# Weighted value sums of three of eight decode samples computed by VectorE, and the value ring cut from three slots to two

## The chip, the cores and the metric

The kernel runs on one core of one Trainium2 chip. The metric is the device time of one launch in microseconds (us); lower is better. Three runs of the kernel before gave 2659.47, 2661.23 and 2663.26 us, so the median is 2661.23 us.

## The reference, cut to what matters

One decoder layer is applied to a prompt of 512 tokens and to eight samples of one new token each. The change touches only the samples' attention over their cached pages:

```python
# D_MODEL 2048, SEQ 512, DEC_BATCH 8, PAST_LEN 1024, PAGE_SIZE 128, SB_HEADS 8, HEAD_DIM 128
k_past = cache_k[i][page_table].reshape(dec_b, past_len, SB_HEADS, HEAD_DIM)
v_past = cache_v[i][page_table].reshape(dec_b, past_len, SB_HEADS, HEAD_DIM)
...
def stick_breaking(q, k, v, sb_bias, q_pos, k_pos):
    z = einsum('bqhd,bkhd->bhqk', q, k) * SB_SCALE + sb_bias
    log_keep = where(causal, log_sigmoid(-z), 0.0)
    after = cumsum(log_keep, axis=3, reverse=True) - log_keep
    a = where(causal, exp(log_sigmoid(z) + after), 0.0)
    return einsum('bhqk,bkhd->bqhd', a, v)
```

For one sample and one head the last line is a sum over 1024 cached positions: weight `a` times the 128 numbers of that position's value row. A page holds 128 positions (one per partition) and eight heads of 128 numbers, so a page in SBUF is 128 x 1024 fp32, 512 KB, and a sample has eight pages. Around it stand the combined input projection, the prompt's attention, a gated position-mixing MLP, the output projection, a SwiGLU feed-forward layer of width 5632 and an embedding gate.

## The kernel before, in words

**Units.** The dense layers are cut into units of 16 weight blocks of 128 x 128. Every block is multiplied in three passes (`x_hi`·`w_hi`, `x_lo`·`w_hi`, `x_hi`·`w_lo`, two halves of 260 tokens each, line 1214). TensorE walks through the units in order. Units 0 to 7 make the queries, 8 to 23 the MLP channels, 24 to 39 keys and values (`U_KV` is 24), from 40 on the output projection follows (`U_OUT` is 40). The feed-forward layer starts at unit 56.

**Turns.** Every other engine has one block of code per unit, in a program order that was written by hand. Below, "turn u" is what an engine does in its loop's round u. VectorE's turn u begins with reading the result tile of unit u-1 (`take`, line 892), for which it waits until TensorE has ended that unit. Then come `low_w` (line 868: the low halves of the weights of unit u+1, without which TensorE can't begin unit u+1), the MLP's or the attention's element-wise steps, and the scoring of cached keys. So TensorE can be ahead of VectorE by at most about one unit. In the even turns of the key and value units VectorE waits for ScalarE's softplus (`soft`, line 958), in the odd ones for TensorE's sums over later positions (line 971).

**Cached keys.** VectorE scores each key page with a product and a reduction (lines 899, 900): three pages per turn in turns 10 to 23, two per turn in turns 24 to 34. The query rows of the next sample arrive by a DMA (`q_rows`) that may be issued only when the last page of the sample before has been scored.

**Cached values.** `V_FIRST = [16, 19, 22, 25, 28, 31, 34, 38]` gives the unit in which the pages of each sample begin: three pages in that unit, three in the next and two in the third. In a unit with three pages `weigh_values` puts them ahead of blocks 7, 11 and 14. It takes each head's 128 x 128 values as the weights of a matmul with one column, eight heads per page, in fp32, which the trace shows as 16 weight loads and 16 matmuls (line 1336). VectorE then reads eight columns of sums out of PSUM at the start of its next turn (`take_values`, lines 937, 940).

**The value ring and GpSimd's queue.** GpSimd issues the loads of value pages. There are three slots: two in `v_ring` and the tile `acc`, which in turn 9 carries the query rows to DRAM. The load of page j waits until page j-3 has been used. GpSimd also squares and adds up finished outputs for the norms (lines 553, 554). Its program is one list, sorted by these keys, and it is worked off strictly in that order:

```python
jobs = [(v_unit(j - V_SLOTS) + 0.8, "load", j) for j in range(V_SLOTS, N_PAGES)]
jobs += [(U_MLP + 3.5 + 2 * i, "mlp", i) for i in range(HEADS)]
jobs += [(U_KV + 3.7 + 2 * i, "attention", i) for i in range(HEADS)]
```

An "attention" job i waits for the head's output. TensorE computes that output in unit 27 + 2i ahead of block 12 (`attend`, lines 1317 and 1321), and ScalarE copies it to `q` (line 660).

Of the kernel before, what the change touches and what calls it, by code (L numbers as in the profile page):

```python
# [26 lines left out]
P = 128  # L27
# [94 lines left out]
V_SLOTS = 3  # L122
# [13 lines left out]
V_UNITS = [u for u in range(V_FIRST[0], V_FIRST[-1] + 3) if v_pages(u)]  # L136
# [27 lines left out]
def build(nc, w_units, x_t, p_t, cache_k, cache_v, page_table, g_mix, g_out, g_ffn, g_ple, g_q, g_k,  # L164
# [3 lines left out]
    with ExitStack() as ctx:  # L168
# [101 lines left out]
        def v_slot(j):  # L270

            return acc[:, :] if j % V_SLOTS == RING else v_ring[:, j % V_SLOTS, :]

        def o_s_ps(u):

            return out_ps[:, 2 * ((tiles_before(u + 1) - 1) % 2) + 1, HALF:HALF + HEADS]
# [68 lines left out]
        v_used = sem("v_used")  # L345
        v_read = sem("v_read")
# [14 lines left out]
        av_ready = sem("av_ready")  # L361

# [19 lines left out]
        def _(sp):  # L382
# [51 lines left out]
            for u in range(U_FFN):  # L434
# [25 lines left out]
                if u == V_UNITS[-1] + 2:  # L460

                    sp.wait_ge(v_used, N_PAGES)
                    sp.dma_start(h[:, H_KEYS:H_PAGES, :], x_t[:, H_KEYS:H_PAGES, :]).then_inc(h_in[1], 16)
# [22 lines left out]
        def _(pool):  # L486
# [112 lines left out]
        def _(act):  # L599
# [71 lines left out]
            def weights_of_sample(u):  # L671

                if u - 1 in SUM_END:
                    b = SUM_END.index(u - 1)
                    act.wait_ge(arg_s_done, b + 1)
                    if b >= 3:
                        act.wait_ge(v_used, PAGES * (b - 2))
# [177 lines left out]
        def _(dve):  # L855
# [73 lines left out]
            def take_values(u):  # L929

                if u not in V_UNITS:
                    return
                b = v_pages(u)[0] // PAGES
                dve.wait_ge(out_done, tiles_before(u + 1))
                sums = q[:, :, PROMPT + b]
                if u == V_FIRST[b]:
                    dve.tensor_copy(sums, o_s_ps(u)).then_inc(v_read, 1)
# [72 lines left out]
            for u in range(1, U_FFN):  # L1010
# [104 lines left out]
                while pages:  # L1115
                    score_next()
                if u > U_OUT_SB:
# [89 lines left out]
        def _(pe):  # L1207
# [117 lines left out]
            def weigh_values(j, u):  # L1325
# [6 lines left out]
                if j == pages[0] and V_UNITS.index(u) > 1:  # L1332
                    pe.wait_ge(v_read, V_UNITS.index(u) - 1)
                for hd in range(HEADS):
                    at = pg * HEADS + hd
                    mm = pe.matmul(o_s_ps(u)[:, hd:hd + 1], v_slot(j)[:, hd * P:(hd + 1) * P],  # L1336
                                   a_s[:, b % 3, at:at + 1], start=False, stop=j == pages[-1],
                                   skip_group_check=True)
                mm.then_inc(v_used, 1)

# [15 lines left out]
            for u in range(1, U_FFN):  # L1356
# [31 lines left out]
                for at, j in zip((14, 11, 7), reversed(v_pages(u))):  # L1388
                    between[at] = lambda j=j, u=u: weigh_values(j, u)
# [148 lines left out]
```

## Time and profile before

| | |
|---|---|
| median of three runs | 2661.23 us |
| the profiled execution's own time | 2663.89 us |
| its span | 2662.3 us |
| TensorE busy | 2623.2 us, 99% |
| VectorE busy | 1218.7 us, 46% |
| ScalarE busy | 781.3 us, 29% |
| GpSimd busy | 158.2 us, 6% |
| chain that ended last | TensorE 95%, VectorE 3%; line 1214 87%, line 1336 4% |

The span is the profiled time from the first to the last instruction of the core, 1.6 us under that execution's own time. Busy shares are means over the whole launch. The change acts only between about 240 and 740 us, so the views that matter are those of this stretch: VectorE's instructions in order of time with the idle time before each, and the same of GpSimd and TensorE. In a row of such a view the first number is the start, the second the duration of the row (several instructions of one kind are merged, with their count at the end), and the bracket says how long the engine sat idle before it and for whom.

### The profile page before, as it was taken

The page shows a single profiled execution, that of the slowest core. Times are in us where ns is not written, and L with a number is a line of the kernel's source. Part 1 is how long each engine was busy: PE and PEld are TensorE (multiplying, and loading weights), DVE is VectorE, ACT ScalarE, POOL GpSimd, SP SyncE. Part 2 cuts the span into 40 slices and gives each one's busy share as a digit, 9 for nine tenths or more (in the row PEclk, how much of TensorE's full clock was granted, in tenths as well). Part 3 has the DMA queues.
Part 4 walks back from the last instruction along what each step waited for, and adds up shares of the span by engine and source line. Part 5 has one row for each costly group of instructions (what it writes and reads, how often), then busy time and mean ns, then how long its engine had stood idle before and what let it go on. Part 6 is the DMA issues. An engine that isn't in the chain of part 4 may idle for free.

```text
span 2662.3 us, 49219 instructions
## 1 busy us (share of the span) xinstructions
PE 2623.2 (99%) x21484; PEld 2600.7 (98%) x21484; DVE 1218.7 (46%) x1400; ACT 781.3 (29%) x912; POOL 158.2 (6%) x170
## 2 busy tenths in 40 slices
PE   7999999999999999999999999999999999999999
PEld 6998999999999999999999999999999999999999
DVE  6368776554456533333333333334343424346443
ACT  5544434444523322222122212121212121224221
POOL 4001111110111200000000000000000000003000
PEclk9998999999999999999999999999999999999999
DMA  4255565554332222222222222222222222222223
GB/s 177 95 190 190 215 237 207 175 186 160 108 128 100 84 96 95 85 91 96 96 82 93 96 80 96 96 96 81 95 96 92 93 86 96 94 83 94 96 86 106
DMA packets 57389, 309.18 MB, mean 116 GB/s; under 512 B 7770, under 2 KB 7770, under 8 KB 30178
## 3 DMA queue, kind: packets, MB, share of 16 engines
q1 hardware_dynamic: 47826, 272.50, 29.0%
q0 software_dynamic: 9216, 33.56, 3.6%
q8 instruction: 177, 2.90, 0.4%
q14 instruction: 26, 0.21, 0.0%
q10 hardware_dynamic: 144, 0.01, 0.0%
HBM read 297.46 MB, written 8.59 MB: 115 GB/s over the span
## 4 chain that ended last, share of the span: by engine, by line
PE 95%; DVE 3%; DMA 1%; ACT 1%; issue 1%; SPq 0%; DVEq 0%; ACTq 0%
PE out_ps L1214 87%; PE out_ps L1336 4%; PE pair_ps L1253 1%; DVE w_lo L868 1%; DVE k_ring L899 0%; PE tok_ps L1321 0%; DVE dot_s L900 0%; DMA q_rows<-q_rows_dram 0%; DMA h<-x_t 0%; ACT x_hi L622 0%; PE pair_ps L1284 0%; PE pair_ps L1303 0%; PE tok_ps L1317 0%; PE pair_ps L1290 0%; PE pair_ps L1299 0%
## 5 line engine op out<-in xcount | busy, mean ns | idle before, releaser
L1214 PE MATMUL out_ps<-x_hi,w_hi 128*128 128x260 f32 x5184 | 1066.9, 287 | 25.8 <-DVE w_lo L868 10.0
L1214 PE MATMUL out_ps<-x_hi,w_lo 128*128 128x260 f32 x5184 | 1048.6, 284 | 0.0
L1214 PE MATMUL out_ps<-x_lo,w_hi 128*128 128x260 f32 x5184 | 1046.8, 284 | 0.0
L1214 PEld LDWEIGHTS out_ps<-x_hi,w_hi 128*128 128x128 f32 x5184 | 805.8, 190 | 31.8 <-DVE w_lo L868 8.9
L1214 PEld LDWEIGHTS out_ps<-x_hi,w_lo 128*128 128x128 f32 x5184 | 803.6, 189 | 0.0
L1214 PEld LDWEIGHTS out_ps<-x_lo,w_hi 128*128 128x128 f32 x5184 | 801.4, 189 | 0.0
L611 ACT ACTIVATE w_hi<-w_raw 128x1024 fp32r<-128x1024 f32 x412 | 411.7, 1047 | 590.2 <-PE out_ps L1214 590.2
L868 DVE TENSOR_TENSOR w_lo<-w_raw,w_hi 128x1024 fp32r<-128x1024 f32 x410 | 501.4, 1255 | 125.1 <-ACT w_hi L611 123.7
L1214 PE MATMUL out_ps<-act_hi,w_lo 128*128 128x260 f32 x1408 | 283.9, 283 | 0.0
L1214 PE MATMUL out_ps<-act_lo,w_hi 128*128 128x260 f32 x1408 | 283.3, 283 | 0.0
L1214 PE MATMUL out_ps<-act_hi,w_hi 128*128 128x260 f32 x1408 | 283.2, 282 | 0.0
L1156 DVE TENSOR_TENSOR h<-h,out_ps 128x520 f32<-128x520 f32 x176 | 122.3, 695 | 228.2 <-PE out_ps L1214 228.1
L1214 PEld LDWEIGHTS out_ps<-act_hi,w_lo 128*128 128x128 f32 x1408 | 217.1, 188 | 0.0
L1214 PEld LDWEIGHTS out_ps<-act_hi,w_hi 128*128 128x128 f32 x1408 | 217.1, 188 | 0.0
L1214 PEld LDWEIGHTS out_ps<-act_lo,w_hi 128*128 128x128 f32 x1408 | 216.6, 188 | 0.0
L1131 DVE TENSOR_TENSOR y_up<-out_ps,h_r 128x520 f32<-128x520 f32 x44 | 30.8, 700 | 295.6 <-PE out_ps L1214 295.6
L1131 DVE TENSOR_TENSOR y_gate<-out_ps,h_r 128x520 f32<-128x520 f32 x44 | 30.8, 700 | 285.0 <-PE out_ps L1214 285.0
L818 ACT ACTIVATE act_hi<-y_up 128x520 fp32r<-128x520 f32 x44 | 28.1, 639 | 428.2 <-DVE y_up L1148 428.2
L815 ACT ACTIVATE y_gate<-y_gate 128x520 f32<-128x520 f32 x44 | 28.1, 640 | 381.5 <-DVE y_gate L1131 381.5
L593 POOL COPY h_sum<-h_sq 128x520 f32<-128x520 f32 x2 | 1.8, 902 | 1543.8 <-ACT h_sq L691 1543.8
L1336 PEld LDWEIGHTS out_ps<-a_s,v_ring 128*128 128x128 f32 x688 | 82.1, 195 | 0.0
L1336 PE MATMUL out_ps<-a_s,v_ring 128*128 128x1 f32 x688 | 80.7, 247 | 0.0
(175 smaller groups left out, 1366.0 us busy)
## 6 DMA issues: line engine op xcount, KB each, us to landing
w_raw<-w_units SPq DMA_DIRECT2D x205, 1024.0 KB, 4.8
k_ring<-cache_k SPq DMA_DIRECT2D x50, 512.0 KB, 5.2
v_ring<-cache_v POOLq DMA_DIRECT2D x43, 512.0 KB, 4.5
acc<-cache_v POOLq DMA_DIRECT2D x21, 512.0 KB, 4.8
k_third<-cache_k SPq DMA_DIRECT2D x14, 512.0 KB, 4.5
h<-x_t SPq DMA_DIRECT2D x4, 1040.0 KB, 9.5
y_t<-h SPq DMA_DIRECT2D x16, 260.0 KB, 6.5
q_rows<-q_rows_dram SPq DMA_DIRECT2D x8, 512.0 KB, 5.4
```

The source lines that it names most:

```text
L593: ins = pool.tensor_copy(h_sum[:, :], h_sq[:, 0, :])
L611: act.activation(w_hi[:, u % 2, cols], w_raw[:, u % 2, cols], ACT.Copy).then_inc(hi_done, 1)
L815: act.activation(y_gate[:, :], y_gate[:, :], ACT.Silu).then_inc(silu_done, 1)
L818: act.activation(act_hi[:, par, g, :], y_up[:, :], ACT.Copy).then_inc(act_hi_done, 1)
L868: dve.tensor_tensor(w_lo[:, u % 2, cols], w_raw[:, u % 2, cols], w_hi[:, u % 2, cols], ALU.subtract).then_inc(lo_done, 1)
L1131: dve.tensor_tensor(halves(dst), tile_ps(t), halves(h_r[:, :]), ALU.mult).then_inc(out_read, 1)
L1156: dve.tensor_tensor(halves(h[:, m, :]), halves(h[:, m, :]), tile_ps(t), ALU.add)\
L1214: mm = pe.matmul(out_ps[:, 2 * (t % 2) + a, 0:HALF], w[:, u % 2, cols], x[:, a * HALF:(a + 1) * HALF], start=first and n == 0, stop=last a ...
L1253: mm = pe.matmul(pair_ps[:, a, 0:HALF], ones[:, :], x[:, a * HALF:(a + 1) * HALF], start=True, stop=True)
L1336: mm = pe.matmul(o_s_ps(u)[:, hd:hd + 1], v_slot(j)[:, hd * P:(hd + 1) * P], a_s[:, b % 3, at:at + 1], start=False, stop=j == pages[-1], s ...
```

## The change

`BY_VECTOR = (1, 3, 5)` names the samples whose value pages VectorE takes. For each of their pages `add_page` multiplies the whole page in place by the weights, which are broadcast over the 128 numbers of a head, and adds it to `acc` (copies it for the first page). It stands at the end of VectorE's turn, behind the last scoring of keys. One unit after the last page, `reduce_values` lets TensorE sum `acc` over the partitions: eight matmuls of one column with `ones`, of the same form as those of a page. `acc` is no longer a slot of the ring, and `V_SLOTS` goes from 3 to 2. The other five samples keep their blocks and units. ScalarE's wait for a free weight tile goes to `v_weighed` where VectorE was the reader.

```diff
-V_SLOTS = 3
+V_SLOTS = 2
...
+BY_VECTOR = (1, 3, 5)
+BY_TENSOR = [b for b in range(SAMPLES) if b not in BY_VECTOR]
+V_UNITS = sorted([(V_FIRST[b] + i, b) for b in BY_TENSOR for i in range(3)] + [(V_FIRST[b] + 3, b) for b in BY_VECTOR])
...
         def v_slot(j):
 
-            return acc[:, :] if j % V_SLOTS == RING else v_ring[:, j % V_SLOTS, :]
+            return v_ring[:, j % V_SLOTS, :]
...
                 if j >= V_SLOTS:
-                    pool.wait_ge(v_used, j - V_SLOTS + 1)
-                elif j % V_SLOTS == RING:
-                    pool.wait_ge(q_rows_out, 16)
+                    before = j - V_SLOTS
+                    if before // PAGES in BY_VECTOR:
+                        pool.wait_ge(v_added, used_by_vector(before))
+                    else:
+                        pool.wait_ge(v_used, used_by_tensor(before))
...
+            def add_page(j):
+
+                b, pg = divmod(j, PAGES)
+                dve.wait_ge(v_in[j % V_SLOTS], 16 * (j // V_SLOTS + 1))
+                values = v_slot(j).rearrange("p (h d) -> p h d", h=HEADS)
+                weights = a_s[:, b % 3, pg * HEADS:(pg + 1) * HEADS].unsqueeze(2).to_broadcast([P, HEADS, P])
+                if pg == 0:
+                    dve.wait_ge(a_s_done, b + 1)
+                    if b == BY_VECTOR[0]:
+                        dve.wait_ge(q_rows_out, 16)
+                    else:
+                        dve.wait_ge(acc_used, BY_VECTOR.index(b))
+                chained(dve.tensor_tensor(values, values, weights, ALU.mult), v_weighed)
+                if pg == 0:
+                    dve.tensor_copy(acc[:, :], v_slot(j)).then_inc(v_added, 1)
                 else:
-                    dve.wait_ge(v_read, V_UNITS.index(u))
-                    dve.tensor_tensor(sums, sums, o_s_ps(u), ALU.add).then_inc(v_read, 1)
+                    dve.wait_ge(v_added, used_by_vector(j) - 1)
+                    dve.tensor_tensor(acc[:, :], acc[:, :], v_slot(j), ALU.add).then_inc(v_added, 1)
...
                 while pages:
                     score_next()
+                for j in v_pages(u):
+                    if j // PAGES in BY_VECTOR:
+                        add_page(j)
...
+            def reduce_values(b, u):
+
+                pe.wait_ge(v_added, used_by_vector(PAGES * b + PAGES - 1))
+                pe.wait_ge(v_read, V_UNITS.index((u, b)) - 2)
+                for hd in range(HEADS):
+                    mm = pe.matmul(o_s_ps(u, b)[:, hd:hd + 1], acc[:, hd * P:(hd + 1) * P], ones[:, 0:1],
+                                   start=False, stop=True, skip_group_check=True)
+                mm.then_inc(acc_used, 1)
...
                 for at, j in zip((14, 11, 7), reversed(v_pages(u))):
-                    between[at] = lambda j=j, u=u: weigh_values(j, u)
+                    if j // PAGES in BY_TENSOR:
+                        between[at] = lambda j=j, u=u: weigh_values(j, u)
+                for b in BY_VECTOR:
+                    if u == V_FIRST[b] + 3:
+                        between[13] = lambda b=b, u=u: reduce_values(b, u)
```

The order of the instructions moves at two places that matter below. VectorE, end of turn 19 and start of turn 20, before (the names: `k_third` is a slot of the key ring, `y` the tile that `take` fills):

```order
L899 TENSOR_TENSOR k_ring<-k_ring,q_rows 128x1024 [waits k_in1,centred]
L900 TENSOR_REDUCE dot_s<-k_ring 128x8 [waits vec_step]
L899 TENSOR_TENSOR k_third<-k_third,q_rows 128x1024 [waits k_in2]
L900 TENSOR_REDUCE dot_s<-k_third 128x8 [waits vec_step]
L937 COPY q<-out_ps 128x8 [waits out_done]
L892 TENSOR_TENSOR y<-out_ps,x_r 128x520 [waits out_done]
```

and of the change at the same place:

```order
L921 TENSOR_TENSOR k_third<-k_third,q_rows 128x1024 [waits k_in2]
L922 TENSOR_REDUCE dot_s<-k_third 128x8 [waits vec_step]
L975 TENSOR_TENSOR v_ring<-v_ring,a_s 128x1024 [waits q_rows_out,a_s_done,v_in0]
L977 COPY acc<-v_ring 128x1024 [waits v_weighed]
L975 TENSOR_TENSOR v_ring<-v_ring,a_s 128x1024 [waits v_in1]
L980 TENSOR_TENSOR acc<-acc,v_ring 128x1024 [waits v_added,v_weighed]
L975 TENSOR_TENSOR v_ring<-v_ring,a_s 128x1024 [waits v_in0]
L980 TENSOR_TENSOR acc<-acc,v_ring 128x1024 [waits v_added,v_weighed]
L914 TENSOR_TENSOR y<-out_ps,x_r 128x520 [waits out_done]
```

Six wide instructions now stand ahead of the next turn's reading of TensorE's tile. The third page uses slot 0 again, which the first page of the same turn has only just left.

GpSimd, around the "attention" job 1 (unit 29), before. The two loads ahead of the job are those of pages 36 and 37 (pages 4 and 5 of sample 4), the load behind it, which goes to the slot `acc`, is that of page 38:

```order
L548 DMA v_ring<-cache_v 128x1024
L543 TENSOR_LOAD table
L543 ISA x2
L548 ISA [waits v_used]
L548 DMA v_ring<-cache_v 128x1024
L553 TENSOR_TENSOR pool_sq<-q 128x512 [waits tok_read]
L554 TENSOR_TENSOR sb_r<-sb_r,pool_sq 128x512 [waits pool_step]
L543 TENSOR_LOAD table [waits pool_step]
...
L548 DMA acc<-cache_v 128x1024
```

and of the change, where the load behind the job is that of page 37:

```order
L567 DMA v_ring<-cache_v 128x1024
L572 TENSOR_TENSOR pool_sq<-q 128x512 [waits tok_read]
L573 TENSOR_TENSOR sb_r<-sb_r,pool_sq 128x512 [waits pool_step]
L560 TENSOR_LOAD table [waits pool_step]
L560 ISA x2
L567 ISA [waits v_used]
L567 DMA v_ring<-cache_v 128x1024
```

Page 37 is the third page of unit 29. Its load has gone from ahead of the job to behind it, since its key is now made from page 35, which belongs to unit 29 itself. The same happens to page 53 in unit 35 (job 4) and to page 61 in unit 39 (job 6).

## Rows read from the trace of the kernel before

**Rows 1.** The page: VectorE's busy tenths in 40 equal slices of the span.

```profile
DVE  6368776554456533333333333334343424346443
```

**Rows 2.** The chain of waits in order of time: start, us, what; one page.

```profile
313.49 1.68 PE out_ps L1336 x16
```

**Rows 3.** VectorE's groups by line and shape, 0 to 760 us: busy, mean ns.

```profile
L899 DVE TENSOR_TENSOR k_ring<-k_ring,q_rows 128x1024 f32<-128x1024 f32 x50 | 61.2, 1224 | 13.3 <-DMA q_rows<-q_rows_dram 9.0 <-DMA k_ring<-cache_k 3.0
...
L977 DVE TENSOR_TENSOR z<-z,causal 128x512 f32<-128x512 f32 x8 | 5.5, 687 | 5.0 <-ACT z L755 3.6 <-ACT z L781 1.4
```

**Rows 4.** VectorE in order of time: first instructions of turns 20 to 22.

```profile
320.69 0.17 DVE L937 COPY q<-out_ps 128x8 f32<-128x8 f32 x1 [3.45 <-PE out_ps L1214]
...
338.68 1.22 DVE L899 TENSOR_TENSOR k_third<-k_third,q_rows 128x1024 f32<-128x1024 f32 x1 [7.57 <-DMA q_rows<-q_rows_dram]
...
341.08 0.16 DVE L940 TENSOR_TENSOR q<-q,out_ps 128x8 f32<-128x8 f32 x1
...
355.69 0.17 DVE L940 TENSOR_TENSOR q<-q,out_ps 128x8 f32<-128x8 f32 x1 [1.10 <-PE out_ps L1214]
```

**Rows 5.** The same view: first instructions of turns 26 to 28.

```profile
428.36 0.17 DVE L937 COPY q<-out_ps 128x8 f32<-128x8 f32 x1 [7.23 <-PE out_ps L1214]
...
447.90 0.17 DVE L940 TENSOR_TENSOR q<-q,out_ps 128x8 f32<-128x8 f32 x1 [2.80 <-PE out_ps L1214]
...
469.49 0.17 DVE L940 TENSOR_TENSOR q<-q,out_ps 128x8 f32<-128x8 f32 x1 [6.36 <-PE out_ps L1214]
```

**Rows 6.** The same view: first instructions of turns 32 to 34.

```profile
553.91 0.17 DVE L937 COPY q<-out_ps 128x8 f32<-128x8 f32 x1 [8.13 <-PE out_ps L1214]
...
573.43 0.17 DVE L940 TENSOR_TENSOR q<-q,out_ps 128x8 f32<-128x8 f32 x1 [0.63 <-PE out_ps L1214]
...
595.52 0.17 DVE L940 TENSOR_TENSOR q<-q,out_ps 128x8 f32<-128x8 f32 x1 [6.66 <-PE out_ps L1214]
```

**Rows 7.** The same view: waits inside turns 26, 27 and 32.

```profile
437.50 1.49 DVE L958 SCALAR_TENSOR_TENSOR keep<-z,soft 128x1280 f32<-128x1280 f32 x1 [3.16 <-ACT soft L669]
...
452.77 1.22 DVE L971 TENSOR_TENSOR z<-z,pair_ps 128x1024 f32<-128x1024 f32 x1 [1.33 <-PE mix_ps L1309]
...
563.63 1.49 DVE L958 SCALAR_TENSOR_TENSOR keep<-z,soft 128x1280 f32<-128x1280 f32 x1 [3.75 <-ACT soft L669]
```

**Rows 8.** A page used by TensorE, GpSimd's next load, landing times of v_ring loads.

```profile
245.86 1.84 PE L1336 MATMUL out_ps<-a_s,v_ring 128*128 128x1 f32 x16
...
248.37 0.59 POOL L548 DMA_DIRECT2D v_ring<-cache_v  x1 [13.50 <-PE out_ps L1336]
...
DMA to landing us min/median/max: 3.4/4.5/8.2
```

**Rows 9.** Unit 29: GpSimd's attention job and next load; TensorE's third page.

```profile
508.85 1.04 POOL L553 TENSOR_TENSOR pool_sq<-q 128x512 f32<-128x512 f32 x1 [20.29 <-ACT q L660]
509.97 1.27 POOL L554 TENSOR_TENSOR sb_r<-sb_r,pool_sq 128x512 f32<-128x512 f32 x1
512.46 0.59 POOL L548 DMA_DIRECT2D acc<-cache_v  x1 [1.22 <-issue]
...
509.41 1.84 PE L1336 MATMUL out_ps<-a_s,v_ring 128*128 128x1 f32 x16
```

**Rows 10.** TensorE in order of time, unit 19: its first and its third page.

```profile
308.69 1.84 PE L1336 MATMUL out_ps<-a_s,acc 128*128 128x1 f32 x16
...
317.27 1.84 PE L1336 MATMUL out_ps<-a_s,v_ring 128*128 128x1 f32 x16
```

**Rows 11.** TensorE in order of time, behind a wait of 4.49 us.

```profile
202.41 2.10 PE L1253 MATMUL pair_ps<-vg,ones 128*128 128x260 f32 x4 [4.49 <-ACT vg L731]
...
208.63 0.42 PE L1214 MATMUL out_ps<-x_lo,w_hi 128*128 128x260 f32 x2
```

**Rows 12.** VectorE in order of time: `low_w` alone, and beside GpSimd's squares.

```profile
326.11 2.36 DVE L868 TENSOR_TENSOR w_lo<-w_raw,w_hi 128x1024 fp32r<-128x1024 f32 x2
...
376.36 4.35 DVE L868 TENSOR_TENSOR w_lo<-w_raw,w_hi 128x1024 fp32r<-128x1024 f32 x2
```

More of the change, by code:

```diff
@@ L133, in v_pages, with used_by_vector, used_by_tensor @@
     return [j for j in range(SAMPLES * PAGES) if v_unit(j) == u]
-V_UNITS = [u for u in range(V_FIRST[0], V_FIRST[-1] + 3) if v_pages(u)]
+BY_VECTOR = (1, 3, 5)
+BY_TENSOR = [b for b in range(SAMPLES) if b not in BY_VECTOR]
+V_UNITS = sorted([(V_FIRST[b] + i, b) for b in BY_TENSOR for i in range(3)] + [(V_FIRST[b] + 3, b) for b in BY_VECTOR])
+V_LAST = V_UNITS[-1][0]
+def used_by_vector(j):
+    return len([i for i in range(j + 1) if i // PAGES in BY_VECTOR])
+def used_by_tensor(j):
+    return j + 1 - used_by_vector(j)
 DIAG = lambda kb: slice(kb * P, (kb + 1) * P)
@@ L929, in take_values @@
             def take_values(u):
[L931 to L937, printed above, removed]
-                else:
-                    dve.wait_ge(v_read, V_UNITS.index(u))
-                    dve.tensor_tensor(sums, sums, o_s_ps(u), ALU.add).then_inc(v_read, 1)
+                for n, (v_u, b) in enumerate(V_UNITS):
+                    if v_u == u:
+                        dve.wait_ge(out_done, tiles_before(u + 1))
+                        sums = q[:, :, PROMPT + b]
+                        if b in BY_VECTOR or u == V_FIRST[b]:
+                            dve.tensor_copy(sums, o_s_ps(u, b)).then_inc(v_read, 1)
+                        else:
+                            dve.wait_ge(v_read, n)
+                            dve.tensor_tensor(sums, sums, o_s_ps(u, b), ALU.add).then_inc(v_read, 1)
+            def add_page(j):
[7 more added lines that the diff above has]
+                        dve.wait_ge(q_rows_out, 16)
+                    else:
+                        dve.wait_ge(acc_used, BY_VECTOR.index(b))
+                chained(dve.tensor_tensor(values, values, weights, ALU.mult), v_weighed)
+                if pg == 0:
+                    dve.tensor_copy(acc[:, :], v_slot(j)).then_inc(v_added, 1)
+                else:
+                    dve.wait_ge(v_added, used_by_vector(j) - 1)
+                    dve.tensor_tensor(acc[:, :], acc[:, :], v_slot(j), ALU.add).then_inc(v_added, 1)
             def weigh_sample(b):
@@ L1331, in weigh_values @@
                 pe.wait_ge(v_in[j % V_SLOTS], 16 * (j // V_SLOTS + 1))
[L1332 to L1333 removed]
+                n = V_UNITS.index((u, b))
+                if j == pages[0] and n > 2:
+                    pe.wait_ge(v_read, n - 2)
                 for hd in range(HEADS):
                     at = pg * HEADS + hd
[L1336 removed]
+                    mm = pe.matmul(o_s_ps(u, b)[:, hd:hd + 1], v_slot(j)[:, hd * P:(hd + 1) * P],
                                    a_s[:, b % 3, at:at + 1], start=False, stop=j == pages[-1],
```

16 lines of the change are left out of this document (11 added, 5 removed).

## The prediction

> **What bounds the kernel now.** I read the page first. TensorE is busy for 99% of the span, so in the mean only what leaves its queue counts. But the change acts between 240 and 740 us, and there VectorE is not idle: slices 4 to 7 of the page (each 66.6 us, so 200 to 466 us) show it six to eight tenths busy, against three or four in the feed-forward layer [rows 1]. That one number makes the page's mean of 46% useless for this question.
>
> So I went to VectorE's instructions in order of time and looked at the first one of each turn, because the bracket there says how long VectorE had nothing to do before TensorE ended the unit. That is the room the change has. In turns 19, 20 and 21, where sample 1's values are summed, the room is 3.45, nothing and 1.10 us [rows 4]. Turn 20 has none because VectorE waits 7.57 us inside it for the next sample's query rows, which come by DMA [rows 4]. In turns 25 to 27 (sample 3) the room is 7.23, 2.80 and 6.36 us [rows 5], in turns 31 to 33 (sample 5) 8.13, 0.63 and 6.66 us [rows 6].
>
> **What the change takes away.** The chain of waits gives 1.68 us of TensorE for a page [rows 2]. 24 of 64 pages leave it, 40.3 us, and three reductions of the same form come back, 5.0 us. If nothing else happened the gain would be 35.3 us. I do not add this number to the sum. It would be right only if TensorE set the pace of these nine units, and the next step shows that it does not.
>
> **What it adds to VectorE's turns.** A page is one multiply and one add of 128 x 1024 fp32 with both inputs in SBUF. The product in the scoring of keys is the same operation and takes 1.22 us [rows 3]. That one input is broadcast does not matter: the broadcast mask over 512 columns takes 0.69 us [rows 3], so 1024 columns would take no more than 1.4. I take 2.45 us for a page. The copy of a first page I leave at the add's price; at half of it a sample would be 0.6 us cheaper.
>
> In a turn with three pages the third one must wait. With two slots, its load can be issued only when the first page has been added. GpSimd starts a load 0.67 us after a page is released (TensorE ends at 247.70, the load starts at 248.37) and it lands 4.5 us later in the median, 3.4 to 8.2 at the ends [rows 8]. That is 5.2 us, and the second page covers 2.45 of it. VectorE idles 2.7 us (1.6 to 6.4 at the ends). A turn with three pages grows by 7.35 + 2.7 = 10.05 us, one with two pages by 4.9, a sample by 25.0.
>
> From then on VectorE sets the pace. `take` of the next turn stands behind the pages, and TensorE can only be one unit ahead: it needs the low weights made in that late turn. The turns add up end to end:
>
> - Sample 1: 25.0 - 3.45 - 0 - 1.10 = **+20.5 us**.
> - Sample 3: 25.0 - 7.23 - 2.80 - 6.36 = 8.6. With turns this late, TensorE's scores and ScalarE's softplus of turn 26, which don't need VectorE's `take`, are ready before VectorE asks. So the 3.16 us wait inside turn 26 goes, and the 1.33 us one in turn 27 too [rows 7]. **+4.1 us**.
> - Sample 5: 25.0 - 8.13 - 0.63 - 6.66 = 9.6, less 3.75 [rows 7] and 1.33 again, 4.5. In turn 31 the third page's load stands behind attention job 2, which waits for TensorE's head in the same unit. I put 2 us on that, between none and 4. **+6.5 us**.
>
> Together +31.1 us. The q_rows wait of 7.57 us stays in full, because `add_page` stands behind the key pages that wait for it and so fills none of it.
>
> **GpSimd beside it.** The squares of attention jobs 0, 2 and 3 (turns 27, 31, 33) now fall beside busy stretches of VectorE. They last 1.04 + 1.27 = 2.3 us [rows 9]. What such company costs is shown by a pair of `low_w`: 2.36 us alone, 4.35 beside GpSimd's squares of the MLP [rows 12]. I take 1 us for each job, **+3 us** (between 0 and 7). The Trainium skill (page "SBUF — State Buffer", section "SBUF: two separate sides") says that the port pair shared by the two engines is an exclusive lock, held for a whole instruction, when VectorE's op has two SBUF inputs and GpSimd's reads SBUF: the other one blocks fully. By that rule the three jobs would cost all of their 7 us if VectorE is always the one that waits, and the total would be 4 us higher. The doubled `low_w` pair agrees with the rule in direction. It also speaks against this change in general: two more two-input operations per page sit on that port.
>
> **The reductions.** Three times 1.68 us of TensorE in units 22, 28 and 34. TensorE has some lead when VectorE's late turns end, but the first page behind them must wait for a slot VectorE has just left (5.2 us after its release, as above). I call it even, **0 us** (between -4 and +5).
>
> **What two slots do to the samples that stay.** A third page's load now waits for the first page of the same unit. From the end of the first page to the start of the third are 317.27 - (308.69 + 1.84) = 6.7 us [rows 10], less 0.67 for GpSimd leaves 6.0 us for a landing of 4.5, at worst 8.2 [rows 8]. In units 16, 17, 22, 23, 28, 34 and 38 I take **+1 us** in all (0 to 6).
>
> Units 29, 35 and 39 are another matter. The load of their third page now has a key behind the attention job of the same unit, as the order in the section on the change shows. That job waits for the head that TensorE computes ahead of block 12, and the page is wanted ahead of block 14. The trace of before has all of it: the job is done at 511.24, the next load starts at 512.46, and TensorE's third page started at 509.41 [rows 9]. So the load starts 3.05 us after the page was wanted. I add a landing of 4.0 us, between 3.4 and the median, since little else is loaded then: 7.05 us of idle TensorE, in a stretch where TensorE is the bound. The other two units have the same spacing. **+21.2 us**.
>
> TensorE then comes back slower. After an idle 4.49 us it ran at half speed from 202.41 to about 208.63 [rows 11], 6.2 us that did 3.1 us of work. Three times 3.1 is **+9.3 us** (0 to 15). At VectorE's turns the same slowing has cover, since TensorE idles there anyway.
>
> **The sum.** 31.1 + 3 + 0 + 1 + 21.2 + 9.3 = 65.6 us on the profiled execution's 2663.9 us, 2729.5. That execution was 2.7 us above the median of its runs, so I forecast 2726.8, say **2727 us**. A measurement of this kernel can tell some 0.2%, 5.3 us, from no change.
>
> **The rivals.**
>
> 1. *VectorE's pages find cover (other side).* TensorE stays the bound of units 19 to 33, VectorE's idle time takes the pages, and 35.3 us go: 2626 us. It decides at the room per turn: 10 us are needed in six turns, 4.9 in three. For it speaks only the page's mean of 46%. Against it, no turn has 10 us of room and turn 20 has none [rows 4 to 6]. Chance 0.03.
> 2. *VectorE as forecast, but no stall in units 29, 35 and 39.* If something lets those loads through before block 14, 21.2 + 9.3 us drop out: 2696 us. Against it stands GpSimd's strict order. Chance 0.13.
> 3. *Loads land late.* Value, key and weight loads meet at the ends of VectorE's turns. If VectorE's six third pages land in 8.2 us and not in 4.5 [rows 8], 6 x 3.7 = 22 us come on top: 2749 us. Chance 0.12.
> 4. *Everything half-hidden, within 5.3 us of before.* It needs rival 2 and some 30 us less from VectorE's turns. Chance 0.02.
>
> My forecast has the remaining 0.70. Its own bounds (landings, port, clock) are about 2705 to 2750. The range that leaves out no more than 2 in 10 takes in rival 2 and most of rival 3: **2694 to 2752 us**. Faster by over 0.2% is rival 1, 0.03; within 0.2% is rival 4, 0.02; slower is the rest, 0.95.
>
> **What would show it.** Right, if in the profile after: no bracket stands before the first instruction of turns 20 to 22, 26 to 28 and 32 to 34; VectorE waits about 3 us for a load of `v_ring` in six places; the wait for `soft` is gone in turns 26 and 32; turns 20 and 21 together last some 50 us in place of the 35.0 between 320.69 and 355.69 [rows 4]; and TensorE shows three waits of about 7 us for a `v_ring` load, with a granted clock of one half behind each. Wrong, if TensorE's idle time stays near that of before, or if the three 7 us waits are missing (then rival 2, and my reading of GpSimd's order was mistaken), or if VectorE's turns do not add up end to end. I would also be wrong if the multiply by broadcast weights took much over 1.2 us: each 0.1 us of it is 2.4 us.

## The result and the profile after

The changed kernel took 2730.06 us (median of 4 runs, 2724.45 to 2731.66) against 2661.61 us of the kernel before (2659.47 to 2663.26). The ratio is 1.0251, with a 95% interval of 1.0238 to 1.0264: **slower by 68 us**, 3 us over the forecast of 2727. The profiled execution took 2729.34 us, its span is 2727.8 us, which is 65.5 us more than the span before. The sum in the prediction was 65.6.

The page after: the engines' totals, the slices and the chain.

```profile
PE 2620.9 (96%) x21148; PEld 2594.9 (95%) x21148; DVE 1278.2 (47%) x1442; ACT 781.3 (29%) x912; POOL 160.9 (6%) x170
...
PE   7999877988999999999999999999999999999999
...
DVE  6368778575445653343334343424243424336533
...
PEclk8998989898999999999999999999999999999999
...
PE 88%; DVE 7%; DMA 3%; issue 2%; POOL 0%; ACT 0%; SPq 0%; POOLq 0%; DVEq 0%; ACTq 0%
```

Some 35 us of TensorE's work left, yet it is busy for 2620.9 us against 2623.2: half clock filled in what the change took out. From 300 to 800 us TensorE worked at half clock for some 60 us, which is 30 us of work (read off windows of 0.5 us). VectorE's slices 7, 9 and 10 rose, from 6, 5 and 4 tenths to 8, 7 and 5 [rows 1], and 7% of the chain is VectorE now, 3% DMA, against 3% and 1%.

VectorE in order of time, from the first value page in turn 19 to the start of turn 22 (start, duration, and in the bracket the idle time ahead):

```profile
317.96 1.22 DVE L975 TENSOR_TENSOR v_ring<-v_ring,a_s 128x1024 f32<-128x1024 f32 x1
319.21 0.69 DVE L977 COPY acc<-v_ring 128x1024 f32<-128x1024 f32 x1
319.82 1.22 DVE L975 TENSOR_TENSOR v_ring<-v_ring,a_s 128x1024 f32<-128x1024 f32 x1
321.07 1.23 DVE L980 TENSOR_TENSOR acc<-acc,v_ring 128x1024 f32<-128x1024 f32 x1
324.07 1.22 DVE L975 TENSOR_TENSOR v_ring<-v_ring,a_s 128x1024 f32<-128x1024 f32 x1 [1.78 <-DMA v_ring<-cache_v]
...
326.48 0.69 DVE L914 TENSOR_TENSOR y<-out_ps,x_r 128x520 f32<-128x520 f32 x1
...
341.65 1.23 DVE L921 TENSOR_TENSOR k_third<-k_third,q_rows 128x1024 f32<-128x1024 f32 x1 [5.09 <-DMA q_rows<-q_rows_dram]
...
350.60 1.23 DVE L975 TENSOR_TENSOR v_ring<-v_ring,a_s 128x1024 f32<-128x1024 f32 x1 [1.68 <-DMA v_ring<-cache_v]
...
353.00 0.69 DVE L914 TENSOR_TENSOR y<-out_ps,x_r 128x520 f32<-128x520 f32 x1
...
371.13 0.69 DVE L914 TENSOR_TENSOR y<-out_ps,x_r 128x520 f32<-128x520 f32 x1
```

The turns begin with the `y<-out_ps` rows, and no bracket stands before them, where [rows 4] had 3.45, nothing and 1.10. A page costs 2.45 us, as forecast. The third page waits 1.78 and 1.68 us for its load.

TensorE in order of time, three of its long waits (units 21, 27 and 29):

```profile
354.42 2.10 PE L1296 MATMUL pair_ps<-vg,ones 128*128 128x260 f32 x4 [11.40 <-ACT vg L753]
...
475.55 2.07 PE L1296 MATMUL pair_ps<-sq,ones 128*128 128x260 f32 x4 [12.30 <-DVE z L1011]
...
538.94 3.57 PE L1380 MATMUL out_ps<-a_s,v_ring 128*128 128x1 f32 x16 [6.45 <-DMA v_ring<-cache_v]
```

And what released it: GpSimd in unit 29, the counterpart of [rows 9].

```profile
531.77 1.03 POOL L572 TENSOR_TENSOR pool_sq<-q 128x512 f32<-128x512 f32 x1 [22.34 <-ACT q L679]
532.88 1.26 POOL L573 TENSOR_TENSOR sb_r<-sb_r,pool_sq 128x512 f32<-128x512 f32 x1
535.36 0.59 POOL L567 DMA_DIRECT2D v_ring<-cache_v  x1 [1.22 <-issue]
```

The load of the third page starts at 535.36, behind the job, and lands 3.6 us later, when TensorE goes on at 538.94. The page then takes 3.57 us instead of the 1.84 of [rows 9]: TensorE is at half speed. Units 35 and 39 repeat it with 6.33 and 6.57 us.

Windows of the turns 19, 20 and 22 (length, busy time of TensorE, its weight loads, VectorE, ScalarE and GpSimd, then TensorE's granted clock, DMA share, GB/s). Before, the clock was 1.00 in all three:

```profile
304.18:326.48 22.30, 20.00 (x161) 19.56 (x159) 20.11 (x23) 10.52 (x12) 4.50 (x4) 1.00 0.62 222
326.48:353.00 26.52, 12.09 (x84) 11.88 (x84) 19.23 (x21) 2.52 (x3) 1.58 (x3) 0.73 0.50 178
...
371.13:390.56 19.43, 17.52 (x126) 17.55 (x127) 13.62 (x26) 3.84 (x5) 2.11 (x4) 0.82 0.65 238
```

**Where the 65.5 us lie.** I cut both traces at the `y<-out_ps` row that opens each of VectorE's turns (at turn 45 it is the `sq<-out_ps` row of the same kind), and subtract. A second trace of the changed kernel (experiment 11) was 2.3 us shorter up to turn 19 and up to 1.5 us off in the other stretches, so a difference of that size in a row of the table can be the execution's own.

| stretch | before us | after us | more | the prediction's terms |
|---|---|---|---|---|
| up to turn 19 | 303.38 | 304.18 | +0.8 | two slots (+1 in all) |
| turns 19 to 21, sample 1 | 52.39 | 66.95 | +14.6 | +20.5 |
| turns 22 to 24 | 53.62 | 54.79 | +1.2 | reduction, 0 |
| turns 25 to 27, sample 3 | 60.18 | 65.13 | +5.0 | +4.1, squares +1 |
| turn 28 | 19.47 | 20.19 | +0.7 | reduction, 0 |
| turns 29 and 30 | 41.61 | 52.75 | +11.1 | stall and clock, +10.2 |
| turns 31 to 33, sample 5 | 64.95 | 70.38 | +5.4 | +6.5, squares +2 |
| turn 34 | 19.58 | 20.15 | +0.6 | reduction, 0 |
| turns 35 and 36 | 41.08 | 52.48 | +11.4 | stall and clock, +10.2 |
| turns 37 to 44 | 100.66 | 110.54 | +9.9 | stall and clock, +10.2 |
| behind the start of turn 45 | 1905.4 | 1910.3 | +4.9 | 0 |

### The profile page after: what moved, and what is told of

It is laid out like the page before. It is cut to its first block, busy times and chain, and to the rows that moved or that the text cites. A ratio compares the mean times of both kernels' runs of the same rounds, so it can differ in the third digit from the quotient of the medians.

```text
span 2727.8 us, 48601 instructions
## 1 busy us (share of the span) xinstructions
PE 2620.9 (96%) x21148; PEld 2594.9 (95%) x21148; DVE 1278.2 (47%) x1442; ACT 781.3 (29%) x912; POOL 160.9 (6%) x170
## 4 chain that ended last, share of the span: by engine, by line
PE 88%; DVE 7%; DMA 3%; issue 2%; POOL 0%; ACT 0%; SPq 0%; POOLq 0%; DVEq 0%; ACTq 0%
PE out_ps L1257 82%; PE out_ps L1380 3%; DMA v_ring<-cache_v 2%; DVE w_lo L890 1%; PE pair_ps L1296 1%; DVE k_ring L921 1%; DVE dot_s L922 1%; DVE x_lo L899 1%; DMA q_rows<-q_rows_dram 1%; DVE v_ring L975 0%; DMA k_ring<-cache_k 0%; PE tok_ps L1364 0%; DMA h<-x_t 0%; DVE y L914 0%; PE tok_ps L1360 0%
```

## Experiments

Each ratio is to runs of the kernel before on the same chip. The experiments ran on three chips, on which the kernel before took 2662.29, 2661.81 and 2663.26 us (2661.61 beside the changed kernel), so differences in us between two kernels carry up to 2 us of that. Diffs are against the changed kernel unless said otherwise.

**1. Only the order of GpSimd's queue mended.** The attention job's key goes from 3.7 to 3.9, so the third page's load stands ahead of the job again.

```diff
-jobs += [(U_KV + 3.7 + 2 * i, "attention", i) for i in range(HEADS)]
+jobs += [(U_KV + 3.9 + 2 * i, "attention", i) for i in range(HEADS)]
```

> The changed kernel with one number changed: the attention jobs of GpSimd get the key 3.9 in place of 3.7, so that each stands behind the page loads of its unit and not ahead of them. Theory A (the strict order of GpSimd's list makes three stalls of TensorE, each with a slow restart): the three waits of 6.3 to 6.6 us for a v_ring load ahead of block 14 go, about 31 us go with them, 2730 becomes about 2700 us, and VectorE's turns stay as long as they are. Rival (two slots are too few by themselves, whatever the order): the waits stay, or move to other pages, and the time stays above 2720 us.

Measured: 2696.3 us (2694.43 to 2699.82), ratio 1.013 (1.0113 to 1.0148), **33.8 us less** than the changed kernel. TensorE's wait is gone. GpSimd in unit 29 of this kernel:

```profile
519.75 0.53 POOL L567 DMA_DIRECT2D v_ring<-cache_v  x1 [14.73 <-PE out_ps L1380]
524.38 0.53 POOL L567 DMA_DIRECT2D v_ring<-cache_v  x1 [4.10 <-PE out_ps L1380]
530.52 0.53 POOL L567 DMA_DIRECT2D v_ring<-cache_v  x1 [5.62 <-PE out_ps L1380]
531.07 1.06 POOL L572 TENSOR_TENSOR pool_sq<-q 128x512 f32<-128x512 f32 x1
```

The loads follow TensorE's releases, the squares come last, and turns 29, 35 and 39 take 24.69, 24.63 and 23.42 us (after: 34.21, 33.70, 33.15). With turns 30 and 36 that is 30.2 us less. Another 3.7 us of the difference between the two traces lie ahead of turn 19, where nothing was changed. Half of the loss is an order in a queue, which a changed number of slots had turned round.

The edit also took the squares away from VectorE's pages. Turns 27, 31 and 33 became 1.8, 2.0 and 1.8 us shorter, but turns 28, 32 and 34 became 1.9, 1.4 and 1.8 us longer. So next to nothing came of it.

**2. The key alone, on the kernel before** (three slots, no pages on VectorE).

> The kernel before, three slots and no pages on VectorE, with only the keys of GpSimd's attention jobs moved from +3.7 to +3.9. Theory A (the key costs and gains nothing by itself; it only matters where a load would stand behind a job whose page is wanted in the same unit): 2660 to 2664 us, turns 29 to 39 as before. Rival: the squares two tenths later are a gain or a loss of their own (over 5 us), and then the 34 us that this key gave back in the changed kernel are not all stalls of the third pages.

Measured: 2663.97 us (10 runs), ratio 1.0 (0.9991 to 1.0009). Turns 29 to 39 are as before. So the key earns nothing by itself where three slots keep the loads ahead; what experiment 1 gave back is the stalls.

**3. Two slots alone, on the kernel before**, with the old key and all pages on TensorE. The one edit is `V_SLOTS = 2`; `v_slot` then never chooses `acc`, since `j % 2` is never `RING`, which is 2.

> The kernel before with V_SLOTS = 2 and nothing else: all eight samples on TensorE, two ring slots, acc unused as a slot. Theory A: four units have an attention job between the first use of a slot and the load of their third page (29, 31, 35, 39); each costs about 10 us, so 2661.6 becomes about 2702 us, and VectorE's turns don't lengthen by themselves. Rival (the stalls in the changed kernel come from VectorE's late turns, which push the loads back): without VectorE's pages no wait for a v_ring load is longer than 2 us and the time stays below 2668 us.

Measured: 2708.93 us (2706.21 to 2718.57), ratio 1.017 (1.0153 to 1.0187). That is 7 us more than I expected, but the stall is there without a single page on VectorE. TensorE in unit 29, and its waits for `v_ring` between 300 and 800 us (sum, times, longest):

```profile
526.37 3.58 PE L1336 MATMUL out_ps<-a_s,v_ring 128*128 128x1 f32 x16 [6.50 <-DMA v_ring<-cache_v]
```

```profile
PE out_ps L1336 <- DMA v_ring<-cache_v: 28.4, 7, 6.6
```

Here four turns are long, 29, 31, 35 and 39 (33.55, 33.12, 32.90 and 33.22 us against 23.88, 23.35, 23.42 and 23.42): unit 31 belongs to sample 5, whose third page TensorE still reads. In the changed kernel that page is VectorE's. The four turns hold 38.7 us. Turns 19 to 27, with three short waits for third pages, took another 9.4.

**4. Two slots and the mended key on the kernel before.**

> The kernel before with two slots and with the attention jobs' key at 3.9, so that page loads go first. The run with two slots alone cost 47 us over before, and its turns 30 to 32 and 36 and 40 carry some 40 of them. Theory A (order) says those go: about 2668 to 2672 us, where the remaining 7 to 10 us are third pages that land late beside key and weight loads in units 17 to 26. Rival (two slots cost by themselves, since a load has only 6 us): more than 2685 us.

Measured: 2670.13 us (8 runs, 2665.45 to 2679.6), ratio 1.0039 (1.0026 to 1.0052). So the missing third slot costs 8 us once the order is right, and 39 us more (2708.93) with the old order.

**5. The pages placed between the key pages.** The turn's first two value pages stand ahead of its last scoring of keys, the third behind it.

```diff
+                values = [j for j in v_pages(u) if j // PAGES in BY_VECTOR]
+                if len(pages) > 1:
+                    score_next()
+                for j in values[:2]:
+                    add_page(j)
                 while pages:
                     score_next()
-                for j in v_pages(u):
-                    if j // PAGES in BY_VECTOR:
-                        add_page(j)
+                for j in values[2:]:
+                    add_page(j)
```

> The changed kernel with VectorE's pages moved inside the turn: the first two value pages stand ahead of the last key page (behind one key page, where more than one is left), the third value page at the end of the turn. The work is the same. Theory B (in the nine turns VectorE's instructions and waits add up end to end and set the pace): the six waits for the third page's load (1.8, 1.7, 2.2, 4.5, 2.5, 2.5 us, 15 in all) and the wait for query rows in turn 20 (5.1 us) are covered by work, so 15 to 20 us go: 2710 to 2715 us. Rival (TensorE or the loads set the pace there, VectorE's waits are only a symptom): less than 5 us change.

Measured: 2713.26 us (2706.27 to 2719.18), ratio 1.0181 (1.016 to 1.0202), 16.8 us less than the changed kernel. VectorE's wait for the third page, of the changed kernel and then of this one:

```profile
DVE v_ring L975 <- DMA v_ring<-cache_v: 15.2, 6, 4.5
```

```profile
DVE v_ring L975 <- DMA v_ring<-cache_v: 4.0, 3, 2.6
```

11 us of waiting went. In turn 20, where the scoring waits for the query rows, two pages now lie in that wait:

```profile
341.61 1.23 DVE L980 TENSOR_TENSOR acc<-acc,v_ring 128x1024 f32<-128x1024 f32 x1
343.35 1.23 DVE L921 TENSOR_TENSOR k_third<-k_third,q_rows 128x1024 f32<-128x1024 f32 x1 [0.52 <-DMA q_rows<-q_rows_dram]
```

The wait fell from 5.09 to 0.52 us. Turns 19 to 21 took 59.7 us in place of 66.95. Turn 34 gave 6 us back (26.18 against 20.15): TensorE waited 0.96 us in it at a value page and was granted half its clock twice, from about 625.5 to 633 and from 639 to 646.5 us, where the changed kernel has one such stretch in this turn.

**6. Both edits together.**

> The changed kernel with both amendments: page loads ahead of the squares, and VectorE's pages split around the last key page. If the two losses are separate, their gains add: 2730 - 34 - 17 = 2679 us. If they are one and the same (late turns that push the loads back, and the other way round), less than two thirds of the sum appear: above 2696 us. It stays above the kernel before in either case, because VectorE's turns still hold some 22 us of page work per sample against 12 us of room.

Measured: 2676.33 us (2673.04 to 2677.24), ratio 1.0053 (1.0037 to 1.007). Against experiment 1 the placing is worth 20.0 us, against experiment 5 the order 36.9: the two gains add. What is left over experiment 4 is 6 us.

**7. No multiply.** VectorE adds the pages of samples 1, 3 and 5 without their weights, so their value sums are unweighted; everything else is computed. ScalarE's wait for a free weight tile goes to `v_added`, since `v_weighed` no longer counts.

```diff
-                chained(dve.tensor_tensor(values, values, weights, ALU.mult), v_weighed)
```

> The changed kernel without the multiply by the weights: VectorE adds the raw pages of samples 1, 3 and 5, so one of the two wide operations per page is left out and the value sums of these samples are not weighted. Theory B (VectorE sets the pace of the nine turns): 24 x 1.22 = 29 us of VectorE's work go; the third page waits for its load longer (its cover is 1.22 instead of 2.45 us), 7 us back, and in turns 25 to 27 and 31 to 33 TensorE becomes the bound before all of it is gained: 2705 to 2712 us. Rival (the stalls of TensorE for value pages hold all of the loss): less than 5 us change.

Measured: 2727.99 us (2723.76 to 2731.62), ratio 1.0246 (1.0225 to 1.0268). **My expectation failed**, and the number lies in the rival's range: 29 us less work for VectorE moved the time by 2. The waits of this kernel, and the windows of its turns 22 and 34:

```profile
DVE acc L979 <- DMA v_ring<-cache_v: 31.5, 6, 6.8
```

```profile
363.41:386.03 22.62, 20.23 (x138) 20.05 (x137) 13.61 (x26) 5.76 (x7) 2.11 (x4) 0.79 0.65 233
...
623.64:652.43 28.79, 27.47 (x180) 26.95 (x180) 12.80 (x17) 9.55 (x10) 3.63 (x6) 0.78 0.43 142
```

The third page's load can't start before the first page is done, and takes its time; without the multiplies VectorE reaches it earlier and waits 31.5 us in place of 15.2. In the six turns with three pages, 5.9 of 22.0 us are left. With the 7.4 us of the three others the nine turns are 13.2 us shorter. That was given back in turns 22, 28 and 34 (22.62, 22.38 and 28.79 us against 19.43, 20.19 and 20.15).

For turn 28 the traces say why. From the start of turn 27 to that of turn 29 it is 40.1 us in the changed kernel, 39.9 without the multiplies, 40.1 without the squares beside them (experiment 1), and 40.0 to 40.1 in experiments 5, 6, 8 and 11. Near the start of turn 27 VectorE's line 1011 lets TensorE go on, and from there TensorE works without a wait until the end of unit 28. The two value pages at the end of turn 27 lie beside that work, and what they cost does not count. The same holds for turns 33 and 34 (40.16, 40.17, 40.21 and 40.11 us in the changed kernel and experiments 1, 6 and 11). Here they took 46.1 us: TensorE waited 1.32 us for a value page in turn 34 and ran at half clock from about 639.5 to 653.5 us. Its granted clock in turns 22, 28 and 34 was 0.79, 0.94 and 0.78. So the operations' price counts in the turns with three pages, where the ring takes back most of what a cheaper one gives, and it does not count at the end of turns 27 and 33.

**8. TensorE kept busy.** 50 useless matmuls in unit 20 and 90 in each of units 21, 27 and 33, where it waits for VectorE, to keep the clock up. They have 200 columns each.

> The changed kernel with useless matmuls (200 columns into a part of PSUM that nobody reads) put where TensorE would idle: 50 ahead of block 10 of unit 20, and 90 ahead of block 6 of units 21, 27 and 33. Theory C: in units 22, 28 and 34 the granted clock was 0.82 to 0.87, which costs 2.5 to 3.5 us each, because TensorE idled for 11 to 12 us before; with the filling the clock stays up, the turns 22, 28 and 34 get shorter by 5 to 8 us together, and the time is 2722 to 2726 us. Rival (the load waits set these units): the clock rises and the turns stay as long as they were, 2728 to 2733 us. If the filling is longer than the idle time, TensorE's unit gets longer and the time rises above 2735 us.

Measured: 2721.39 us (2719.99 to 2725.67), ratio 1.023 (1.0213 to 1.0247), 8.7 us less. The number lies just below my expectation, but the trace does not carry the reason. From the start of turn 19 to turn 45 it takes 513.3 us, the changed kernel 513.4. Turn 20 with its clock at 0.92 in place of 0.73 is 1.3 us longer, and turn 22 is no better:

```profile
326.60:354.40 27.80, 22.41 (x182) 22.06 (x181) 19.17 (x21) 3.24 (x5) 1.58 (x3) 0.92 0.49 171
...
371.07:390.80 19.73, 17.84 (x128) 17.67 (x127) 13.61 (x26) 4.33 (x5) 2.11 (x4) 0.83 0.67 234
```

Only turn 34 gained (17.86 against 20.15 us, clock 0.94 against 0.87). What the profiled run gained as a whole lies ahead of turn 19 (2.4 us) and behind turn 45 (6.4 us), where nothing was filled.

The filling did not do what it was there for. In turns 22 and 28 a stretch at half clock stayed, 373.5 to 381 and 506.5 to 514 us, as long as in the changed kernel (372.5 to 380, which begins at a wait of 2.26 us ahead of the unit's first page, and 505.5 to 513). In turns 33 and 34 such stretches went or shrank, and these two turns took 37.2 us in place of 40.2. That is a sign that the clock does cost time there; what turns 22 and 28 lose by it this run can't tell.

**What lowers the clock in turns 28 and 34.** I had put it down to the idle 11 to 12 us of the unit before. The traces of the changed kernel show something else. These are the reduction and the third page of unit 28, and the granted clock around them, then that of turn 34:

```profile
502.83 1.84 PE L1390 MATMUL out_ps<-ones,acc 128*128 128x1 f32 x16
...
505.34 2.90 PE L1380 MATMUL out_ps<-a_s,v_ring 128*128 128x1 f32 x16
```

```profile
491.05:505.50 14.45, 14.45 (x128) 14.45 (x126) 13.14 (x23) 6.82 (x9) 1.59 (x3) 1.00 0.73 255
505.50:512.30 6.80, 6.80 (x35) 6.80 (x35) 1.74 (x4) 1.15 (x2) 0.53 (x1) 0.53 0.66 228
634.37:649.00 14.63, 14.63 (x129) 14.63 (x128) 12.64 (x15) 6.00 (x6) 1.59 (x3) 1.00 0.75 253
649.00:655.80 6.80, 6.80 (x35) 6.80 (x35) 1.13 (x4) 1.45 (x2) 0.53 (x1) 0.52 0.20 77
```

TensorE was back at full clock for 14 us and did not idle once. The clock fell to half just when the third page began, one weight block behind the reduction. In all seven traces with three samples on VectorE half clock begins in unit 28 within some 2 us of that page's start. In unit 34 it does in all but experiment 7, where the clock was low before. The kernels without a reduction in unit 28 (before, experiments 2, 3, 4, 9 and 10) have no half clock in that turn. In unit 22 it came in experiments 5, 6 and 7 and not in the others, so it does not come each time. Some 6.8 us at half clock are 3.4 us of TensorE's work; in experiments 5, 6, 7, 8 and 11 some stretches lasted only half as long. No run moved the reduction away from the pages, so it is not shown that their standing together is the cause.

**9. One sample where there is more room.** Only sample 6 (units 34 to 36) on VectorE, two slots, mended key; to be compared with experiment 4.

> Only sample 6 goes to VectorE (its pages fall in turns 34 to 36, and turns 35 and 36 score no keys), with page loads ahead of the squares. In the trace of before VectorE's room ahead of turns 35, 36 and 37 is 2.94, 10.70 and 1.37 us. Theory B: what counts is the room of each turn. Turn 34 (10.1 us of pages and load wait against 2.9 of room plus 3 us of waits that vanish) runs over by about 4 us, turn 35 just fits, turn 36 runs over by 2 to 3, while TensorE saves 8 x 1.68 - 1.68 = 11.8 us. With the 0 to 8 us that two slots cost the other samples this comes to 2655 to 2668 us, the same as before. Rival (any page on VectorE costs more than it saves, as for samples 1, 3 and 5 with 3 to 15 us each): above 2672 us.

Measured: 2670.51 us (6 runs), ratio 1.0036 (1.0022 to 1.0049), the same as the 2670.13 of experiment 4, although TensorE has 7 x 1.68 = 11.8 us less to do. It lies between the two ranges that I had given, so neither is borne out. Turn 34 lost 5.5 us, turn 35 won 3.7, turn 36 lost 1.4. TensorE waited 7.59 us in turn 35 and 3.23 us in turn 37, each time for line 1011 of VectorE, behind the turns with three and with two pages.

**10. The same a unit later** (`V_FIRST` 35 for sample 6).

> Two slots and the mended order as in the run with 2670 us; only sample 6 goes to VectorE, and its pages begin in unit 35, where turn 35 had 10.7 us of room and turn 37 5.7, and not in unit 34, whose turn still scores keys. Theory A (a page on VectorE is worth its 1.68 us of TensorE exactly where the turn has room for it): 7 x 1.68 = 11.8 us less than 2670, so 2658 us, 2656 to 2663. Rival B (the three pages of turn 36, with 1.4 us of room, push turn 37 by some 7 us, which TensorE feels): 2663 to 2670.

Measured: 2667.01 us (12 runs, 2664.24 to 2674.3), ratio 1.0018 (1.0008 to 1.0027). The time and the late turn are the rival's. Turns 34 and 35 are 7 us shorter together than in experiment 4, turns 36 and 38 4 us longer each. TensorE's only wait from 598 to 722 us, and the windows around and behind it:

```profile
PE pair_ps L1296 <- DVE z L1011: 7.5, 1, 7.5
```

```profile
641.00:653.50 12.50, 9.76 (x71) 8.55 (x69) 10.12 (x20) 2.00 (x2) 1.12 (x2) 0.99 0.40 133
653.50:663.50 10.00, 5.20 (x20) 4.84 (x21) 6.11 (x9) 6.71 (x8) 0.53 (x1) 0.50 0.69 261
663.50:690.50 27.00, 27.00 (x220) 26.25 (x219) 17.45 (x15) 12.49 (x13) 4.51 (x6) 1.00 0.48 159
690.50:698.00 7.50, 7.50 (x37) 7.43 (x37) 2.11 (x5) 2.42 (x3) 0.53 (x1) 0.54 0.21 70
```

The pages at the end of turn 36 make the next turn's `z` (line 1011) late. That line reads `pair_ps`, and TensorE may not fill `pair_ps` again in the middle of unit 37 before it is read. TensorE waits 7.5 us, goes on at 658.30 and is at half clock for another 5 us (1.00 there in experiment 4). The clock is full again for 27 us, and then half from 690.5 to 698, right behind the reduction of sample 6 (687.45) and the third page (689.96) of unit 38, with no wait ahead of it. By my estimate from these rows, half of the time at half clock is lost, so the wait and the two stretches come to 7.5 + 2.6 + 3.5 = 13.6 us of TensorE. That is more than the 11.8 us. No version here beats the kernel before.

**11. The changed kernel once more.**

> The changed kernel once more, for a second trace: up to turn 45 the same within 2 us (817 us). If the 5 us by which the part behind turn 45 was longer than in the kernel before are an execution's own, that part comes out anywhere between 1904 and 1911 us; if they belong to the changed kernel, it is 1910 again.

Measured: 2726.32 us in one run. Turns 19 to 44 take 514.6 us (513.4 in the first trace), and the part behind 1908.3 (1910.3). So the sum of the table's stretches from turn 19 to 44 repeats within 1.2 us, and the trace leaves the 4.9 us behind turn 45 unexplained. In all traces that part took between 1903.9 us (experiment 8) and 1910.3. The kernels with three samples on VectorE show 1908 to 1910 but for experiment 8, the others 1904 to 1908, and the code of that part is the same. That stays open.

## Why the prediction was right, step by step

**What bounds.** Right in the main: in all nine places no bracket is left before the first instruction of the turn. My sentence that TensorE can be ahead "by at most about one unit" because of the low weights was too generous. TensorE's longest waits are in the middle of a unit, at `pair_ps`. In unit 21 its input was late (11.40 us), in unit 27 VectorE had not yet read the tile (12.30 us). So the turns with three pages add up as I wrote. The pages of turns 27 and 33 stand behind the instruction for which TensorE waits and are not on the path (experiment 7). A missing bracket ahead of a turn did not show that.

**The price of a page** was 2.45 us with a multiply of 1.22, as taken. The copy was the term with a choice, and I chose the add's price; it took 0.69 us. The Trainium skill (page "VectorE: DVE Perf Modes", section "The perf-mode tier table") gives an fp32 copy in SBUF twice the rate of an operation on two tensors, and the trace roughly agrees with 0.69 against 1.22, 1.8 times.

**Sample 1, +20.5, measured +14.6.** The term that was most mis-sized. Three parts make 4.9 of the 5.9 us: each third-page wait 1.78 and 1.68 us in place of 2.7 (1.9 together), the copy (0.5), and the query rows' wait, which I let "stay in full": 7.57 us became 5.09 (2.5). The rows are issued when the sample before is scored, and the late turn gave them time. The last 1.0 us is in small items, among them a wait of 0.28 us for ScalarE that went. So turns 20 and 21, for which the prediction had "some 50 us", took 44.65.

**Samples 3 and 5, +4.1 and +6.5, measured +5.0 and +5.4** with the squares in them. With 1 and 2 us of squares the prediction had 5.1 and 8.5, so sample 5 was 3.1 us too dear. The waits for `soft` vanished as forecast. The third-page waits were 2.16 and 4.51 us, then 2.48 and 2.55. In turn 26 the load took 6.2 us to land. In turn 31 I had put 2.7 + 2 us, since the load stands behind attention job 2. It did start 1.7 us late, but it landed in 3.6 us, and the operation beside the squares was longer and covered more of it.

**GpSimd's squares, +3.** Each of the three jobs lengthened VectorE's operations by some 1.8 us, 5.4 in all, within the bounds of 0 and 7. Little of that reached the total: without this company (experiment 1) turns 27 and 28 together took 40.13 us against 40.06, and turns 33 and 34 took 40.17 against 40.16. Turn 27 of the changed kernel:

```profile
485.70 1.95 DVE L980 TENSOR_TENSOR acc<-acc,v_ring 128x1024 f32<-128x1024 f32 x1
487.57 2.30 DVE L975 TENSOR_TENSOR v_ring<-v_ring,a_s 128x1024 f32<-128x1024 f32 x1
489.90 1.23 DVE L980 TENSOR_TENSOR acc<-acc,v_ring 128x1024 f32<-128x1024 f32 x1
```

```profile
485.30 1.27 POOL L572 TENSOR_TENSOR pool_sq<-q 128x512 f32<-128x512 f32 x1 [12.86 <-ACT q L679]
486.64 2.14 POOL L573 TENSOR_TENSOR sb_r<-sb_r,pool_sq 128x512 f32<-128x512 f32 x1
```

Two operations of 1.22 us took 1.95 and 2.30, and GpSimd's took 1.27 and 2.14 in place of 1.04 and 1.27 [rows 9]. Both engines wait in turn. The lock of the Trainium skill's page "SBUF — State Buffer" (section "SBUF: two separate sides"), under which one of the two blocks fully, fits: together they lose 1.8 + 1.1 us, while 2.3 us on VectorE alone would have needed it to be always the one that waits.

**Reductions and two slots, 0 and +1, measured +3.3** (up to turn 19, turns 22 to 24, 28 and 34). I wrote that at VectorE's turns the slowing of the clock "has cover, since TensorE idles there anyway". It has not: in turn 27 TensorE goes on at 475.55, at half clock until about 479, and is the bound from there to the end of unit 28. I also put the reductions at nothing. They take 1.84 us each, and in units 28 and 34 some 7 us at half clock begin right behind them with TensorE busy all the while (rows under experiment 8). Both costs lie inside the 40.1 us of turns 27 and 28, which took 41.05 us in the kernel before.

**The three stalls, +21.2, measured 19.3** (6.45, 6.33, 6.57 us against 7.05 each, since in unit 29 the load started 2.9 us after the page was wanted and not 3.05, and landed in 3.6 us and not in 4.0). **The slow restart, +9.3, measured 12.9**: turns 29, 35 and 39 grew by 30.3 us, so 11.0 on top of the waits, and turns 30 and 36 by another 1.9. This step carried half of the forecast, and experiments 1, 2 and 3 show its cause: the order in GpSimd's list, made by `V_SLOTS` in the key of a load. Rival 2 without these stalls was priced at 2696; the kernel without them took 2696.3.

So that the total of 65.6 met 65.5 is luck. Samples 1 and 5 were 9.0 us too dear. Against that, 4.9 us behind turn 45 were not foreseen, the reductions and two slots were 2.3 us too cheap and the stalls with their restart 1.8. By the medians of all runs the loss is 68.4 us. The kind of each loss, VectorE's three-page turns and the order of GpSimd's list, was forecast and is shown by the experiments.

## What to carry to other kernels

A work list sorted by keys that are computed from a buffer count changes its order when the count changes: print the order again and look for a load that now stands behind a job which waits for the same stage. When work moves to an engine that is idle on average, add up its idle time per turn, and also find the first thing in the next turn that the bound engine needs in mid-stage: a sample's 11.8 us of TensorE bought nothing as long as one turn was 7 us late. Work that needs no data from a wait belongs ahead of the instruction that waits (17 to 20 us here). Before you make an operation cheaper, look whether it stands ahead of the instruction that the bound engine waits for or behind it. In turns 27 and 33 it stood behind, and nothing came of the cheaper operation.

## What the runs showed that I had not expected

- Cutting a cost of 29 us on the engine that seemed to set the pace gained 2 us (experiment 7): the loads of a two-slot ring and the lead of TensorE behind it each took their part.
- TensorE's clock fell to half without any idle time before it. It did so behind a reduction and a value page that stand one weight block apart, 32 weight loads with one column each (rows under experiment 8, and 690.5 to 698 us in experiment 10).
- After one wait of 7.5 us TensorE was at half clock for another 5 us (experiment 10).
- A load of 512 KB into `v_ring` landed in a median of 3.7 us in the changed kernel, against 4.5 before [rows 8]. In turns 19 and 20 it was 3.5 and 3.4, which is why the third pages waited 1.7 us there and not 2.7. The DMA engines moved 203 GB/s in place of 240 between 304 and 391 us; that the load is faster for this reason is not shown, and one load in turn 26 took 6.2 us.
